# Expert sums of a PEER block: two slots of 64 tokens per gathered tile, column-half matmuls, groups unrolled

## The reference, cut to what matters

```python
def peer_experts(xn, w_query, sub_keys, expert_u, expert_v):
    ...
        qr = (xb @ w_query).astype(f32).reshape(PEER_BLOCK, PEER_HEADS, 2, PEER_KEY_HALF)
        s1 = jnp.einsum('thd,hnd->thn', qr[:, :, 0], keys1)
        s2 = jnp.einsum('thd,hnd->thn', qr[:, :, 1], keys2)
        v1, i1 = lax.top_k(s1, PEER_TOPK)
        v2, i2 = lax.top_k(s2, PEER_TOPK)
        ...
        sc, ci = lax.top_k(cand, PEER_TOPK)
        ...
        gate = jax.nn.softmax(sc, axis=-1)
        hid = jnp.einsum('thkd,td->thk', expert_u[eid], xb, preferred_element_type=f32)
        act = jax.nn.gelu(hid, approximate=False) * gate
        return jnp.einsum('thk,thkd->td', act, expert_v[eid].astype(f32)).astype(xb.dtype)
```

## Time and profile before

| | us |
|---|---|
| median of 3 runs | 4086.36 |
| lowest, highest | 4086.21, 4100.81 |
| span of the profiled execution | 4090.1 |
| PE busy | 3315.7 (81%) |
| DVE busy | 2191.8 (54%) |
| POOL busy | 2278.2 (56%) |
| ACT busy | 992.4 (24%) |
| gathers, share of 16 DMA engines | 71.6% |

### The profile page before, as it was taken

The page is one execution under the profiler, slowest core; times in us unless marked ns, Lnnn a source line. Parts: engine busy times, 40 slices in busy tenths (PEclk is TensorE's granted clock), DMA queues, the critical chain, the costliest instruction groups (busy, mean ns, idle before and its releaser), DMA issues.

```text
span 4090.1 us, 38210 instructions
## 1 busy us (share of the span) xinstructions
PE 3315.7 (81%) x11032; PEld 1816.9 (44%) x11032; DVE 2191.8 (54%) x4881; ACT 992.4 (24%) x2278; POOL 2278.2 (56%) x2189
## 2 busy tenths in 40 slices
PE   8997757897788787887879778877888687969999
PEld 4444535453444344443535344444545253534444
DVE  1124285567444854477456744486357644574543
ACT  2112213222222132212221222212221222213332
POOL 0000055667556775767566755676566656666764
PEclk9998778898889897898889888898899798989999
DMA  3321187899789998899889978899799979999996
GB/s 125 118 75 63 39 298 263 309 363 389 264 302 335 362 358 289 316 346 365 280 313 373 365 269 297 318 360 342 278 324 369 356 260 322 352 364 373 381 355 243
DMA packets 413927, 1214.00 MB, mean 297 GB/s; under 512 B 43680, under 2 KB 137888, under 8 KB 413600
## 3 DMA queue, kind: packets, MB, share of 16 engines
q0 software_dynamic: 294912, 1073.87, 71.6%
q1 hardware_dynamic: 118816, 137.66, 9.9%
HBM read 1190.61 MB, written 20.77 MB: 296 GB/s over the span
## 4 chain that ended last, share of the span: by engine, by line
PE 54%; DVE 14%; issue 13%; DMA 7%; POOL 5%; ACT 4%; another core or an unknown queue 2%; SPq 1%; POOLq 0%; DVEq 0%; ACTq 0%
PE expert_sum L894 28%; PE bank L894 23%; DVE u_rows L1645 5%; DMA u_rows<-in_peer_u_dram,group_ids 4%; DMA w_query<-in_peer_w_query_dram 3%; PE bank L897 3%; POOL u_rows L576 3%; POOL v_rows L576 2%; ACT weight_diagonals L610 1%; ACT L610 1%; ACT arena L610 1%; DVE arena L1420 1%; DVE arena L1552 1%; DVE arena L1537 1%
## 5 line engine op out<-in xcount | busy, mean ns | idle before, releaser
L894 PE MATMUL expert_sum<-v_rows,weight_diagonals 128*128 128x512 f32 x4096 | 1871.7, 617 | 153.0 <-ACT weight_diagonals L610 116.9
L576 POOL DMA_INDIRECT v_rows<-in_peer_v_dram,group_ids x1024 | 1191.1, 1163 | 827.7 <-PE expert_sum L894 541.8
L1645 DVE CUSTOM_DVE_ANT_0 u_rows<-u_rows,ffn_in 128x1024 f32<-128x1024 f32 x1024 | 1215.7, 1225 | 454.8 <-DMA u_rows<-in_peer_u_dram,group_ids 410.3
L894 PEld LDWEIGHTS expert_sum<-v_rows,weight_diagonals 128*128 128x128 f32 x4096 | 810.4, 200 | 1161.7 <-issue 1078.0
L576 POOL DMA_INDIRECT u_rows<-in_peer_u_dram,group_ids x1024 | 1052.3, 1028 | 416.8 <-issue 371.0
L897 PE MATMUL bank<-constants,arena 128*128 128x128 f32 x968 | 184.5, 336 | 330.2 <-DVE arena L1475 82.4
L610 ACT ACTIVATE weight_diagonals<-constants,expert_weight 128x128 f32<-128x128 f32 x1024 | 331.7, 390 | 228.5 <-PE expert_sum L894 177.4
L894 PE MATMUL bank<-w_query,arena 128*128 128x256 f32 (+1 forms) x1088 | 297.6, 436 | 87.4 <-DMA w_query<-in_peer_w_query_dram 50.6
L610 ACT ACTIVATE gelu<-hidden 128x8 f32<-128x8 f32 x128 | 26.7, 208 | 1386.1 <-DVE hidden L1645 1237.0
L897 PEld LDWEIGHTS bank<-constants,arena 128*128 128x128 f32 x968 | 139.1, 171 | 392.6 <-issue 212.2
L894 PEld LDWEIGHTS bank<-w_query,arena 128*128 128x128 f32 x1088 | 231.6, 215 | 155.7 <-issue 59.6
(11 more groups left out here) (166 smaller groups left out, 1968.1 us busy)
## 6 DMA issues: line engine op xcount, KB each, us to landing
w_query<-in_peer_w_query_dram SPq DMA_DIRECT2D x64, 1024.0 KB
u_rows<-in_peer_u_dram,group_ids POOLq DMA_INDIRECT x1024
v_rows<-in_peer_v_dram,group_ids POOLq DMA_INDIRECT x1024
w_channel<-in_w_in_dram SPq DMA_DIRECT2D x12, 512.0 KB
conv_scratch<-conv_out SPq DMA_DIRECT2D x12, 512.0 KB, 2.6
arena<-conv_scratch SPq DMA_DIRECT2D x8, 768.0 KB
tok_scratch<-token_out SPq DMA_DIRECT2D x8, 648.0 KB
arena<-tok_scratch SPq DMA_DIRECT2D x8, 648.0 KB
```

The costliest lines, as they stand in the source:

```text
L576: nc.gpsimd.indirect_dma_start(ring[:, j, :], None, table, bass.IndirectOffsetOnAxis(ids[:, half, j:j + 1], 0)).then_inc(landed[j], 16)
L894: return nc.tensor.matmul(out_, lhsT, rhs, start=start, stop=stop, **kw)
L1645: v.tensor_tensor_reduce(u_ring[:, j, :], u_ring[:, j, :], xb[:], 1.0, 0.0, ALU.mult, ALU.add, hid[:, g * G + j:g * G + j + 1]).then_inc(u ...
```

## The change

**Pairing.** A gathered tile j now holds, for one half b = j % 2 of the tokens, two slots: slot 2i of 64 tokens in partitions 0 to 63 and slot 2i + 1 of the same tokens in partitions 64 to 127. Two gathers (b = 0, 1) cover two slots of 128 tokens, as before. The diagonal is 128 x 64 (two 64 x 64 diagonals stacked), and its matmul contracts over both slots into half b of `acc`'s partitions; b alternates between successive matmuls. Number and width of the value-sum matmuls stay (16 per group, 512 columns).

**Placing ids, gates and rows.** The ids, gates and normed rows must be put in that order: PE multiplies with columns of the identity into banks 4, 5 and 0 to 3 (`to_pairs`, `rows_to_pairs`), and ACT copies out. `xb` becomes two tiles of 1024, ids and gates have two buffers; POOL's copies of ids and DVE's copies go.

**Weights.** DVE builds the diagonals, four tiles per instruction, in two halves per group; ACT's 1024 diagonals go, and gelu is taken in two halves.

**Order.** All groups are unrolled (no `Fori` in the expert stage), the pieces are cut anew (15 of them), PE runs piece g before the sums of group g, DVE puts the second half of the weights at marks (`fill`) inside its pieces. `fill` on PE does nothing. Piece by piece the front now has: 0 the first transposes and norms, 1 the decays, 2 the heads' transposes and first products, 3 and 4 two levels each of the triangular inverse, 5 its last level and the state, 6 the attention's norms and DeltaNet's output, 7 logits and softmax, 8 the output projection, residual and norm, 9 to 12 PE's four pairs of query columns, whose top 16 DVE takes in pieces 10 to 13, 13 and 14 also the picks of ids (`pick`) and the gates; group 15 has none. Beside tile 0's experts pieces 0 and 1 stand in group 2 and pieces 7 and 8 in group 8. The arena shrinks by 4 KB a partition; `mixT` and `onehot` share other buffers.

```diff
-V_STEPS = 99
-V_FIRST = 16
-FIRST = 2
+NP = NT * NG
 EARLY = 2 * TOPK // G
+B = 64
+NB = P // B
+PAIRS = G // NB
+GP = G // 2
...
+    c[:, C_REP:C_REP + B] = row % B == col[:, :B]
...
+            def gather_u(q, pair):
+                if q:
+
+                    pool.wait_ge(u_used, (q - 1) * G + 2 * pair + 2)
+                    pool.sem_inc(wait_carrier)
+                for j in range(2 * pair, 2 * pair + 2):
+                    nc.gpsimd.indirect_dma_start(
+                        u_ring[:, j, :], None, table_u, bass.IndirectOffsetOnAxis(id_of(q, j), 0)).then_inc(u_landed[j], 16)
+
+            def gather_v(q, pair):
+                if q:
+
+                    pool.wait_ge(v_used, (q - 1) * PAIRS + pair + 1)
+                    pool.sem_inc(wait_carrier)
+                for j in range(2 * pair, 2 * pair + 2):
+                    nc.gpsimd.indirect_dma_start(
+                        v_ring[:, j, :], None, table_v, bass.IndirectOffsetOnAxis(id_of(q, j), 0)).then_inc(v_landed[j], 16)
+
+            for q in range(NP):
+                e, g = divmod(q, NG)
+                if q == 0 or q == EARLY or (e and g == 0):
+
+                    pool.wait_ge(ids_ready, 1 if q == 0 else e + 2)
+                    pool.sem_inc(wait_carrier)
+                for pair in range(PAIRS):
+                    gather_u(q, pair)
+                for pair in range(PAIRS):
+                    gather_v(q, pair)
...
+            def take_rows(t):
+
+                for b in range(NB):
+                    if t:
+
+                        act.wait_ge(u_used, t * SLOTS - NB + b + 1)
+                    for n in range(2):
+                        act.wait_ge(rows_mm, 2 * NB * t + 2 * b + n + 1)
+                        nc.scalar.copy(xb[:, b, n * 512:n * 512 + 512], bank[2 * b + n][:, :]).then_inc(rows_ready, 1)
+
+            def experts(q):
+
+                for half in range(2):
+                    cols = slice(half * GP, half * GP + GP)
+                    act.wait_ge(u_used, q * G + cols.stop)
+                    f(gel[:, q % 2, cols], hid[:, q % 2, cols], ACT.Gelu).then_inc(gelu, 1)
...
+            def to_pairs(dst, src, cols):
+
+                for b in range(NB):
+                    for s in range(NB):
+                        last = mm(dst[s * B:s * B + B, cols.start + b:cols.stop:NB], ident[:, b * B:b * B + B],
+                                  src[:, cols.start + s:cols.stop:NB])
+                return last
...
+            def rows_to_pairs(t):
+
+                pe.wait_ge(xb_ready, t + 1)
+                pe.wait_ge(scores_ready, NQ * (t + 1))
+                for b in range(NB):
+                    for n in range(2):
+                        for s in range(NB):
+                            last = mm(bank[2 * b + n][s * B:s * B + B, :], ident[:, b * B:b * B + B],
+                                      xb_new[:, n * 512:n * 512 + 512])
+                        last.then_inc(rows_mm, 1)
...
+            def expert_slots(q):
+
+                t, g = divmod(q, NG)
                 if g == 0:
-
-                    pe.wait_ge(h2_ready, t * 2)
-
+                    add_h1(t)
+                for pair in range(PAIRS):
+                    for b in range(NB):
+                        pe.wait_ge(v_landed[pair * NB + b], (q + 1) * 16)
+                    pe.wait_ge(diag_ready, 2 * q + (pair * NB) // GP + 1)
                     for n in range(2):
-                        last = mm(acc[:, n * 512:n * 512 + 512], ident, h1[:, n * 512:n * 512 + 512], True, False)
-                    last.then_inc(h1_added, 1)
-                for j in range(G):
-                    pe.wait_ge(v_landed[j], (t * NG + g + 1) * 16)
-                    pe.wait_ge(diag_ready, t * SLOTS + g * G + j + 1)
-                    for n in range(2):
-                        last = mm(acc[:, n * 512:n * 512 + 512], diag[:, j, :], v_ring[:, j, n * 512:n * 512 + 512],
-                                  False, g == NG - 1 and j == G - 1)
+                        for b in range(NB):
+                            last = mm(acc[b * B:b * B + B, n * 512:n * 512 + 512], diag[:, q % 2, pair * NB + b, :],
+                                      v_ring[:, pair * NB + b, n * 512:n * 512 + 512], False,
+                                      g == NG - 1 and pair == PAIRS - 1)
                     last.then_inc(v_used, 1)
...
+            for q in range((NT - 1) * NG):
+                t = q // NG + 1
+                for i in front_piece(q):
+                    pieces[i](t)
+                if q == 1:
+                    ids_to_pairs(3, rest)
+                    pe.wait_ge(vector_front, 1)
+                    gates_to_pairs(rest)
+                if q % NG == NG - 2:
+                    ids_to_pairs(2 * t + 3, whole)
+                    pe.wait_ge(vector_front, t + 1)
+                    gates_to_pairs(whole)
+                if q % NG == NG - 1:
+                    rows_to_pairs(t)
+                expert_slots(q)
...
+            def expert_weights(q, half):
+
+                e, g = divmod(q, NG)
+                cols = slice(half * GP, half * GP + GP)
+                dve.wait_ge(gelu, 2 * q + half + 1)
+                v.tensor_tensor(act_w[:, q % 2, cols], gel[:, q % 2, cols], gate[:, e % 2, g * G + cols.start:g * G + cols.stop],
+                                ALU.mult).then_inc(weights_ready, 1)
+                dve.wait_ge(weights_ready, 2 * q + half + 1)
+                if q >= 2:
+
+                    dve.wait_ge(v_used, (q - 2) * PAIRS + (half + 1) * PAIRS // 2)
+                v.tensor_tensor(diag[:, q % 2, cols, :], cst[:, C_REP:C_REP + B].unsqueeze(1).broadcast_to([P, GP, B]),
+                                act_w[:, q % 2, cols].unsqueeze(2).broadcast_to([P, GP, B]), ALU.mult).then_inc(diag_ready, 1)
+
+            def expert_dots(q):
+                e, g = divmod(q, NG)
+                if g == 0:
+
+                    dve.wait_ge(gates_out, e + 2 if e else 1)
+                if q == EARLY:
+                    dve.wait_ge(gates_out, 2)
                 for j in range(G):
-                    dve.wait_ge(u_landed[j], (t * NG + g + 1) * 16)
-                    v.tensor_tensor_reduce(u_ring[:, j, :], u_ring[:, j, :], xb[:], 1.0, 0.0, ALU.mult, ALU.add,
-                                                hid[:, g * G + j:g * G + j + 1]).then_inc(u_used, 1)
-                dve.wait_ge(gelu, t * NG + g + 1)
-                v.tensor_tensor(act_w[:, g * G:g * G + G], gel[:, g * G:g * G + G], gate[:, g * G:g * G + G], ALU.mult).then_inc(weights_ready, 1)
+                    if g == 0 and j < NB:
+
+                        dve.wait_ge(rows_ready, 2 * NB * e + 2 * j + 2)
+                    dve.wait_ge(u_landed[j], (q + 1) * 16)
+                    v.tensor_tensor_reduce(u_ring[:, j, :], u_ring[:, j, :], xb[:, j % NB, :], 1.0, 0.0, ALU.mult, ALU.add,
+                                           hid[:, q % 2, j:j + 1]).then_inc(u_used, 1)
+
...
+            def second_half(q):
+
+                yield
+                expert_weights(q, 1)
+                yield
+
+            pending = iter(())
+
+            def fill(n):
+
+                for _ in range(n):
+                    next(pending, None)
 
             def experts_out(t):
```

354 lines of the change are left out of this document (179 added, 175 removed).

## The result

Over 20 executions of each, side by side, the changed kernel took 4123.95 us (median; 4100.05 to 4160.42) and the kernel before 4082.33. The ratio is **1.0105** (95% interval 1.0079 to 1.0131): slower, beyond the 0.5% bound. I had forecast 3840 with a range of 3740 to 3985.

The account below looks back on a forecast made before the run. PE, busy 81%, and the DMA engines were both taken as near their end, in a ring of waits. From 4090.1 us, six stretches saved 233, first stretch 5, last tile 4, tail 7: 3841, say 3840; range 3740 to 3985.

Parts of the forecast that it names:

- the pieces' length: Front pieces beside the experts: taken from tile 0's bare front, pieces 0 to 7 lasting 5.3 to 16.6 us, piece 8 26.1.
- the table's 398.9: Middle tiles: sum over 16 groups of the longer of DVE or PE time and gather time, 398.9 us a tile.
- one stall of unknown cause: State update: DVE's 8.4 us wait, once in each of four tiles, kept, making a tile 407 us against 445.8.
- I costed POOL at nothing: POOL's gather issues: same 2048 gathers, 18.6 us a group, under the 21.2 of the gathers, so no cost.
- The value sums: PE's expert sums: two column halves overlap fully, 6.95 us a group instead of 13.9.
- The gathers: DMA in the expert stage: 8.39 MB a group at 396 GB/s, 21.2 us, more with query weights or next tile's loads.
- the rival 372: Rival on gathers: DMA holds only 372 GB/s, a tile takes 422 us, time 3930; chance 0.25.
- First stretch: First stretch with experts beside a front, 435.7 us before: -5 us, bounds -20 and +20.
- Last tile: Last tile's experts, without a front: bound by gathers, -4 us.
- Tail: Tail after the last tile's experts: one group of sums shorter, -7 us.
- the slower one: Rival in pieces 9 to 12: PE waits for query weights, holding back sums and v gathers; 4200 us; chance 0.07.
- Little changes: Rival in middle tiles: gathers at 0.90 already full beside a front, a tile 436 us, time 4015; chance 0.06.

Follow-up runs that it names:

- e4: The changed kernel with PE's old order, sums of group g - 1 ahead of piece g; 3724 us, 0.963 of the kernel before, updates on time.
- e12: The changed kernel with two chained memsets of 64 elements on POOL behind every gather; 4406 us, 1.077 of the kernel before, late set.
- e13: The changed kernel with six chained memsets on POOL behind every fourth gather; 4263 us, 1.043 of the kernel before, late set.
- e10: The changed kernel with gathers of 2 KB instead of 4 KB a row from the second group on; 4031 us, 0.985, late set.
- e11: The changed kernel with every value sum added twice on PE; 4228 us, 1.035 of the kernel before, late set.
- e17: The changed kernel with two chained memsets of 64 elements on POOL behind every second gather; 4214 us, 1.089, on time.

## Why the prediction was wrong

| group | forecast | old order on time (e4) | changed, late |
|---|---|---|---|
| 0, 1 | 25.7, 21.5 | 21.6, 21.1 | 25.1, 21.8 |
| 2 to 5 | 21.3, 23.0, 21.4, 27.5 | 21.7, 21.3, 21.7, 25.4 | 29.8, 27.4, 32.0, 36.9 |
| 6 to 9 | 23.7, 26.9, 33.0, 21.2 | 23.1, 25.4, 32.0, 18.8 | 23.1, 26.1, 40.5, 19.1 |
| 10 to 12 | 25.2 each | 28.1, 29.0, 25.7 | 28.2, 29.0, 26.5 |
| 13 to 15 | 31.2, 21.2, 25.7 | 30.5, 20.6, 25.1 | 37.4, 20.5, 26.4 |

**The step that failed** is the pieces' length: "Its bare length is shown by tile 0's front, which runs with nothing beside it". That front runs ahead of nearly all gathers, where no update is late. Beside them groups 2 to 5 (the inverse, where PE, DVE and ACT hand over most often) took 126.1 us instead of the forecast 93.2, and groups 8 and 13 took 7.5 and 6.2 more; these six are 46.6 of the 50.8 us by which a tile exceeded the table's 398.9. In e4, on time, groups 2 to 5 took 90.1.

**The sign was in front of me.** Rows 8 had a stall of 8.4 us "<- remote" that I kept as one stall of unknown cause. The matmul that it waits for ended at 1163.51 us in one tile, and its update came at 1170.77, 7.26 later: it is a late update. (Those of two sums that ended later, at 1167.22 and 1169.18, came right behind it, at 1170.83 and 1170.88: PE's updates were held up together and came in order.) I should have asked what else it would meet if POOL's issues moved: I costed POOL at nothing because 18.6 us of issues fit under 21.2. They do fit; but now they stand in one run, beside the inverse.

**The value sums** held: forecast 6.95 a group, measured 7.09 on time (PE's timeline, 32 records), a factor 1.96. In the late profile 1041.2 us in all instead of 940, at a clock of 0.79.

```profile
1454.71 7.09 PE L911 MATMUL expert_sum<-v_rows,weight_diagonals 128*64 128x512 f32 x32
```

The Trainium skill's 2.38 for three column tiles (TensorE: Matmul & The Clock Gate, § Measured speedup vs the span model), from which I had estimated 8.8, does not carry over to these two halves.

**The gathers** held where updates are on time: 377 GB/s and DMA at 0.99 over a whole tile, 394 over the last tile (forecast 396; the rival 372). The Trainium skill's 358 GB/s per core (DMA: Bandwidth & Descriptors, § Specifications) is below all of these.

**The sum where updates are on time.** There it would have erred the other way: e4 took 3724 us, 116 under the forecast, with 391 us a tile instead of 407 and 348 in the last tile instead of 376. And e4's gain on the kernel before in its set is 144 us, not the forecast 249: I took the base, 4090, from a trace with late updates and the pieces from a stretch without them, so part of the forecast gain was late updates that the change does not remove.

**First stretch**: forecast -5, measured +50.6 late; in e4 441.9 us, +6. Groups 2 and 8 hold two pieces there, not 0, 1 and 8 as the prediction has it. Of the 44.4 us between the two kernels 34.4 are in groups 3 to 6, which hold pieces 2 to 5, as groups 2 to 5 do in the other stretches: again the inverse. **Last tile**: forecast -4, measured -17.4; sized too small. **Tail**: forecast -7, measured -5.0.

**The rivals**: the slower one had the right sign and another mechanism. PE did not wait for `w_query` at length (72.4 us in all, against 50.6 in the kernel before), and groups 10 to 12 came within 4 us. "Little changes" came out nearest in the tile (436 forecast, 449.7 measured), for another reason than full gathers: DMA was at 0.89. Of my signs for wrong, the last one came: DMA below 0.93 with DVE waiting inside pieces, pieces longer beside gathers than bare.

What is shown: late updates occur in both kernels, in the changed one over three times as long on average (1.67 and 0.47 us). In a set without them the same code is 332 (half rows), 295 (sums twice) and 467 us (old order) faster, the kernel before 215 (4082 against 3867). So the change gives back more in the late sets than it gains. That late updates depend on POOL's pace is shown by e12 and e13, that bytes don't matter by e10, that the lower clock doesn't make them by e11 (late at 0.886) and e4 (on time at 0.822). That they are all of the difference between the sets is argued, from the same busy times, the same packet times and e13 beside e17. Open: what differs between sets, by what way POOL's issues hold PE up (its updates or the matmuls themselves), and the changed kernel's own time on time.

## What to carry to other kernels

A stage that is made faster can take a brake away: ask what it releases (here POOL's gathers), and whether that then runs in one block beside code that lives on handoffs between engines. Take the length of such code from a stretch with the same neighbours, not from one where it runs alone. A wait that a profile puts down to nothing ("remote" on a single core) is a mechanism still to be found, and it scales with the change until shown otherwise. An update that is missing from a trace looks like a late one: confirm a delay by the start of the engine that waits. And a gain of a few per cent is worth running on several chips or at several times before it is believed.

## What the runs showed of the hardware

- A semaphore update from PE can arrive 3 to 4 us after the matmul's modelled end (mean), with waits of DVE or ACT up to 11.5 in the changed kernel, while POOL issues indirect DMAs every 1.24 us for more than six in a row; at 1.47 and 1.93 us an issue in turn it doesn't (e12: 0.02). DVE's (0.09) and ACT's (0.01) hardly do. Halving the bytes changes nothing (e10: 1.76). It occurs in some sets of runs and not in others, for the same kernel, and the kernel before is 5 to 6.5% slower there (3867; 4073 to 4120).
- POOL leaves 0.3 us between two indirect DMAs; a memset of 0.17 us fits in for 0.03, and a second one behind it brings 0.2 to 0.7.
- Two column halves at 512 float32 columns overlap nearly in full (7.09 us for what takes 13.9 in line).
